# A two-block fp32 transformer on one core: 512-token products in the ordinary weight tiles, and another order of one piece of VectorE's work

## What is computed

```python
def conv_ffn(x, w_up, conv_w, conv_b, w_down):
    S = x.shape[1]
    h = x @ w_up
    ...
    return (jax.nn.silu(g) * u) @ w_down

def odd_mixer(x, w_in, w_out, lq1, lk1, lq2, lk2, sub_g, rel_bias, layer):
    bsz, S, _ = x.shape
    h = x @ w_in
    q, k, v = jnp.split(h, 3, axis=-1)
    ...
    return o @ w_out
```

## Time and profile before

| | us |
|---|---|
| median of 3 runs | 2655.42 (2654.74 to 2657.49) |
| the profiled execution, its own time | 2659.59 |
| its span, first to last instruction | 2657.8 |
| TensorE busy | 2580.7 (97%) |
| VectorE busy | 1541.4 (58%) |
| ScalarE busy | 1265.5 (48%) |
| mean granted TensorE clock | 0.989 |

### The profile page before, as it was taken

How to read it: one execution, slowest core, us unless ns; L and a number is a source line. 1 busy time by engine, 2 the same in 40 slices (tenths; PEclk the granted TensorE clock), 3 DMA queues, 4 the chain that set the end, 5 groups by cost and what they waited for, 6 DMA issues and landing times.

```text
span 2657.8 us, 51025 instructions
## 1 busy us (share of the span) xinstructions
PE 2580.7 (97%) x20838; PEld 2380.9 (90%) x20838; DVE 1541.4 (58%) x2598; ACT 1265.5 (48%) x2097; POOL 118.3 (4%) x185
## 2 busy tenths in 40 slices
PE   8999999999999999999999999989999999999998
PEld 8985999999995699999989777779966998999998
DVE  5234666653688776664467898952475445444433
ACT  4336344432457654442365887742475243444422
POOL 0000000000000000000001233300000000000000
PEclk9999999999998999999999999999999999999999
DMA  7950233333321123333354666633311331333232
GB/s 196 116 84 1 64 104 96 96 104 106 101 96 64 32 80 96 96 96 121 102 198 136 193 203 184 199 102 96 96 48 57 100 123 49 96 99 98 95 104 72
DMA packets 75787, 279.04 MB, mean 105 GB/s; under 512 B 9402, under 2 KB 11610, under 8 KB 75088
## 3 DMA queue, kind: packets, MB, share of 16 engines
q1 hardware_dynamic: 62112, 217.42, 25.7%
q0 software_dynamic: 13488, 58.88, 10.0%
HBM read 267.03 MB, written 9.24 MB: 104 GB/s over the span
## 4 chain that ended last, share of the span: by engine, by line
PE 81%; DVE 11%; ACT 4%; issue 2%; DMA 1%; POOL 0%; DVEq 0%; SPq 0%; ACTq 0%
PE acc L376 63%; PE acc L407 3%; PE acc L565 2%; DVE big L2165 2%; DVE res_tmp L2464 1%; PE ps L407 1%; PE ps L565 1%; PE acc L2013 1%; DVE big L2795 1%; DVE w_lo L348 1%; PE acc L1665 1%; DVE big L1817 1%; DMA res_tmp<-scratch_rows 1%; DVE res_tmp L2458 1%; PE ps L741 1%
## 5 line engine op out<-in xcount | busy, mean ns | idle before, releaser
L376 PE MATMUL acc<-x_split,w_hi 128*128 128x256 f32 x7424 | 1152.8, 277 | 5.4 <-DVE big L2165 3.3
L376 PEld LDWEIGHTS acc<-x_split,w_hi 128*128 128x128 f32 x7424 | 984.6, 188 | 8.0 <-issue 7.4
L376 PE MATMUL acc<-x_split,w_lo 128*128 128x256 f32 x3712 | 724.3, 277 | 0.0
L348 DVE TENSOR_TENSOR w_lo<-w_raw,w_hi 128x1024 fp32r<-128x1024 f32 x389 | 474.8, 1221 | 384.0 <-ACT w_hi L342 384.0
L342 ACT ACTIVATE w_hi<-w_raw 128x1024 fp32r<-128x1024 f32 x389 | 410.2, 1055 | 559.8 <-PE acc L376 517.7
L376 PEld LDWEIGHTS acc<-x_split,w_lo 128*128 128x128 f32 x3712 | 560.0, 188 | 0.0
L376 PE MATMUL acc<-big_r,w_hi 128*128 128x256 f32 x3376 | 521.5, 276 | 0.8 <-DVE big_r L2848 0.8
L376 PEld LDWEIGHTS acc<-big_r,w_hi 128*128 128x128 f32 x3376 | 446.1, 188 | 1.7 <-DVE big_r L2848 1.0
L376 PE MATMUL acc<-big_r,w_lo 128*128 128x256 f32 x1688 | 328.7, 276 | 0.0
L376 PEld LDWEIGHTS acc<-big_r,w_lo 128*128 128x128 f32 x1688 | 254.1, 188 | 0.0
L1344 ACT ACTIVATE res_tmp<-acc,par 128x512 f32<-128x512 f32 x84 | 64.9, 773 | 136.0 <-PE acc L376 131.5
(11 more groups left out here) (392 smaller groups left out, 3142.7 us busy)
## 6 DMA issues: line engine op xcount, KB each, us to landing
w_raw<-in_stream SPq DMA_DIRECT2D x405, 512.0 KB, 3.6
res_tmp<-scratch_rows POOLq DMA_DIRECT2D x96, 320.0 KB, 5.2
big<-scratch_rows POOLq DMA_DIRECT2D x32, 320.0 KB, 5.7
scratch_bias<-res_tmp POOLq DMA_DIRECT2D x8, 320.0 KB, 13.6
res_tmp<-in_x SPq DMA_DIRECT2D x2, 1024.0 KB, 6.9
res_tmp<-scratch_bias POOLq DMA_DIRECT2D x8, 256.0 KB, 4.1
scratch_x<-res_tmp POOLq DMA_DIRECT2D x1, 2048.0 KB, 8.1
scratch_kv<-big POOLq DMA_DIRECT2D x1, 2048.0 KB, 9.1
```

The costliest lines, as they stand in the source:

```text
L348: dve.tensor_tensor(w_lo[:, u.slot], w_raw[:, u.slot], w_hi[:, u.slot].bitcast(F32), ALU.subtract).then_inc(lo_done, 1)
L376: mm = pe.matmul(a[:, h], w, AR[:, x + k, h], start=(k == 0 and w is wh and x == hi and h.start == 0), stop=(k == total - 1 and w is wl), ...
```

## The change

1. In `product_tile` each term is one matmul of all 512 tokens in place of two of 256.
2. In `strassen_dve`, behind the last pair, the three additions come first and the four splits behind them.

```diff
@@ -360,7 +360,7 @@
 
             pe.wait_ge(acc_free[t.bank], t.in_bank + 1)
             a, k, total = acc[t.bank], 0, sum(blocks)
-            parts = [slice(at, at + HALF) for at in range(0, n, HALF)]
+            parts = [slice(0, n)]
             for m in blocks:
                 pe.wait_ge(lo_done, u.count + 1)
                 for b in range(m):
@@ -670,8 +670,8 @@
                 else:
                     for n in range(3):
                         add(n)
+                    for n in range(RING):
                         split_lo(dve, st_unit(stage, pairs) + n)
-                    split_lo(dve, st_unit(stage, pairs) + 3)
```

## The result

The changed kernel takes **2699.55 us** (median of 5 runs, 2699.26 to 2702.75) against 2657.2 us before (median of 5 runs beside it, 2654.74 to 2657.94): ratio 1.017, 95% interval 1.0159 to 1.0181. It is slower by 42 us, where 80 us less were forecast. The profiled execution has a span of 2697.8 us at a granted clock of 0.992.

The account below looks back on a forecast made before the run. TensorE, chiefly matmul line L376, was taken to bound the kernel. Terms of -80 (512-column products), -2 (slow pieces), +2 (scan waits) and 0 us (additions first) sum to -80 us: 2575 us from 2655.4, range 2566 to 2610.

Parts of the forecast that it names:

- What bounds the kernel: Whole span: TensorE bounds, with 81% of the chain; the ordinary tile's matmul L376 alone is 63%, 1674 us.
- PEld was to fall to about half: Long L376 stretches: weight loading should fall from full to about half or less, if the loads have room.
- I take 215.8 ns (213.3 + 2.5), the value nearest to those rows.: L376's 512-column product: 215.8 ns instead of 226.7 for two of 256, judged by plain fp32 rows; -80 us.
- 7385 terms: L376's terms that count on the chain: 1674 us / 226.7 ns, out of 8100 terms in all.
- the load has to fit between two starts: L376 at 256 columns: weight load and stream, about 107 ns each, must take turns, giving the 113.3 ns pace.
- The upper bound of 226.7 ns: L376's 512-column product: at most 226.7 ns, reached if the surplus grows with the columns.
- The second pace of 117.8 ns: 192 L376 products from 714.24 us, 11.1 ns over their columns; losing that excess was forecast at -2 us.
- I expect half of it to go: State-space scan, 1420 to 1770 us: half of a 3.3 us gain goes to the next waits; +2 us.
- Part 2: VectorE before the attention: additions first only fill a 1.89 us wait for ScalarE; 0 us, between 0 and +0.2.
- The slower one: Every L376 term: load and stream of 512 no longer overlap, 326.6 ns, about 3393 us; chance 4%.
- The surplus belongs to every product: L376: 6.7 ns surplus per product whatever its length, 220.0 ns for 512; gain 49 us, 2608 us; chance 17%.
- The rule of N / 2.4 + 2.5 ns: Skill's issue gap for TensorE matmuls: 215.8 ns for 512, taken for L376; its 109.2 for 256 contradicted the trace.

Follow-up runs that it names:

- e4_addresses: TensorE-only program with weights shifted 0 to 192 numbers from the activations: in the kernel's order, 512 columns take 233.3 ns at 16, 227.0 at 0.
- e6_256_unshifted: The kernel before, with the 16 numbers of padding between activations and weights removed: 2759.96 us, ratio 1.0397 to the kernel before.
- the rows at shift 0: TensorE-only rows of 96 products with weights a multiple of 64 numbers behind the activations: fp32r 119.8 ns for 256 columns, 227.0 for 512.
- (16,16): TensorE-only rows with activations and weights both moved by 16 fp32 numbers: 227.0 ns for 512 columns, 119.8 for 256.
- (16,32): TensorE-only rows with activations moved by 16 and weights by 32 fp32 numbers: 233.3 ns for 512 columns, 113.6 for 256.
- the sweep: TensorE-only rows in the kernel's order of terms at 22 weight shifts from 0 to 60 numbers: best 226.8 ns for 512, 113.5 for 256.

## Why the prediction was wrong

- **What bounds the kernel: right.** TensorE and L376 make 81% and 64% of the chain, and the time went where the price of a term went. ScalarE's waits for L376 from 350 to 660 us are 137.3 us (72.0 + 65.3), where they were 140.6. One sign was missed: PEld was to fall to about half of the long stretches, and fell to 80% (248.36 of 309.88 us).
- **The failed step: "I take 215.8 ns (213.3 + 2.5), the value nearest to those rows."** The term measured 233.3. At 7385 terms that is 17.5 ns x 7385 = 129 us, which is more than the whole miss of 122 us (42 + 80). Two errors are in that step. First, the small surplus of plain fp32 was carried over to fp32r, for which no row had it. These rows were misread too, as products of 216 and 429 ns: they are halves of products that leave two records each, and the count of records was not set beside the count of calls. That miscount alone doesn't explain the miss, because each half has a weight load and a surplus of 2 to 3 ns of its own. Second, the explanation made for them ("the load has to fit between two starts") was fitted to four numbers and never had a row of its own; a load of a quarter of the length made 512 no faster. In its place the runs showed that the surplus of an fp32r product goes with the distance between the weights and the activations, and is 20.0 ns for 512 at the kernel's distance.
- **The upper bound of 226.7 ns was no bound.** It came from scaling 6.7 ns with the columns, and the text excluded more only by the same plain rows. The surplus at this place is 6.7 ns for 256 and 20.0 for 512. It is no property of the instruction, so neither a fixed nor a proportional rule could carry it over.
- **The second pace of 117.8 ns was the clue, and was read wrongly.** It showed that one shape with operands of one kind can have two surpluses. I took that as support for the load. `e4_addresses` has this pace in rows of 256 whose neighbours or order are other. With the distance at 0 the second pace is gone: the piece of 22.61 us takes 23.04 in `e6_256_unshifted`, 120.0 ns like every long piece there. So it belongs to the same dependence; which neighbour sets it in this tile was not shown. In the changed kernel the piece became 22.39 us, and the long ones grew.

```profile
746.15 23.04 PE acc L376 x192
```

- **The sum with the right price.** 7385 x (233.3 - 226.7) = +49 us; 42 were measured. The slow pieces gave back a little, and the stretch below took up some 8 us. The span grew by 40.0 us in the profiled execution. Of that growth, 9.0 us fell from 984 (now 996) to 1770 (now 1791) us, where L376's busy time grew by 17.3. This stretch holds the scan, where others wait for each other too: TensorE's waits for L2464, 21.4 us before, are 18.9. The forecast had this as "I expect half of it to go": there half of a gain, here about half of a loss went to others' waits. The mechanism stands, with the sign turned.
- **Part 2: right.** 0 us forecast, ratio 1.0004 measured, 3.57 us to L1817 both times.
- **The rivals.** The slower one (4%) named a point that holds by arithmetic: slower from 13.4 ns of surplus on, and 20.0 were measured. Its mechanism, a load wholly behind the stream, would have been 326.6 ns and isn't what happens. "The surplus belongs to every product" comes nearest to the rows at shift 0, but is neither exact nor of the right size (11.7 to 16.0 ns from 256 to 512 columns, where it said 6.7). No rival had an address in it.
- **The rule of N / 2.4 + 2.5 ns.** The bf16 rows follow N / 2.4 + 2.5 to 0.1 ns at 128, 256 and 512 columns. The fp32r rows don't at any place tried (227 to 234 for 215.8). The rule is the Trainium skill's, "TensorE: Matmul & The Clock Gate", section "Back-to-back issue gap"; it names no type, and the 215.8 ns taken for fp32r are its figure for 512.

What stays open is why the relative place matters. In fp32r the pace at full clock depends on the difference between where the weights and where the activations begin, and differently for two lengths; weights are loaded while the product before still streams. At the lower clock only the kernel's own place was seen. A clash of the two reads in the memory could do all that, but this is argued and not shown. The Trainium skill, "TensorE: Matmul & The Clock Gate", section "Step-by-step: what each phase is for", says that TensorE reads through two independent ports, one for the stream and one for the weights. No run here shows the ports. If the clash is the cause, two ports alone don't keep the two reads apart: (16,16) and (16,32) differ by 6.3 ns for 512. Whether bf16 has bad places too wasn't tried; its rows were all at one shift.

## What to carry to other kernels

Fewer, longer products are not cheaper by themselves: before you merge them, measure the pace of the new shape in a row of its own, in the same type and with the operands where the kernel has them. When one shape shows two paces in a trace, find out what differs between the two before you extrapolate from either. And a tuned padding belongs to the shape it was tuned for: 64 bytes turned this same change from +42 us to -97 us.

## What the runs showed of the hardware that I had not expected

- The pace of fp32r products at full clock depends on the distance between weights and activations modulo 256 bytes: 226.8 to 234.2 ns for 512 columns and 113.5 to 121.7 ns for 256 in the sweep. For 256 columns the order of the operands and what ran ahead matter as well (113.5 or 117.8 ns at one distance). The place that is best for 256 (64 bytes) is among the worst for 512.
- At 1.2 GHz and the kernel's own distance no surplus is left: 426.7 ns for 512 columns, the columns alone.
- fp32r products of 128 and 192 columns take 111.1 and 111.5 ns, so there is a floor near 111 ns at distance 0; bf16 of 128 columns takes 55.8.
- A plain fp32 product leaves two records, and its two halves together take 858 ns for 512 columns, 3.8 times the fp32r product.
